# Mixture-of-experts stage: expert groups ordered from both ends of the load order, with odd pass counts and one shared turn

## The chip, the cores and the metric

The kernel runs on one core of one Trainium2 chip. The metric is the device time of one execution in microseconds (us), the median of several runs. All operands are 32-bit floats.

## The reference

A trunk of two layers (DEPTH = 2) works on 128 context tokens and 512 latent tokens, 640 in all, of width 1024. Each layer has a mixer (attention, a state-space scan, neighbourhood attention) and a channel sub-layer. The change lies in the channel sub-layer only, whose reference is:

```python
s = jax.nn.sigmoid((t @ p["w_router"]).astype(jnp.float32))
_, idx = lax.top_k(s + p["b_router"].astype(jnp.float32), TOP_K)          # 4 of 32 experts
sel = jnp.take_along_axis(s, idx, axis=-1)
w = sel / jnp.sum(sel, axis=-1, keepdims=True) * ROUTE_SCALE
gates = jnp.einsum("nk,nke->ne", w, jax.nn.one_hot(idx, N_EXPERTS))
hg = jnp.einsum("nd,edf->nef", t, p["w_e_gate"])                          # d = 1024, f = 128
hu = jnp.einsum("nd,edf->nef", t, p["w_e_up"])
routed = jnp.einsum("nef,efd->nd", jax.nn.silu(hg) * hu * gates[:, :, None], p["w_e_down"])
shared = (jax.nn.silu(t @ p["w_s_gate"]) * (t @ p["w_s_up"])) @ p["w_s_down"]
```

A layer has 640 x 4 = 2560 assignments of a token to an expert. How they fall follows from the drawn inputs. If the 32 experts of a layer are sorted by their number of tokens and taken four at a time, the most loaded expert of each four (its lead) has, from the reference's own routing:

| rank of the group | 0 | 1 | 2 | 3 | 4 | 5 | 6 | 7 |
|---|---|---|---|---|---|---|---|---|
| lead's tokens, layer 0 | 176 | 121 | 109 | 84 | 69 | 59 | 48 | 37 |
| lead's tokens, layer 1 | 274 | 123 | 104 | 77 | 67 | 58 | 49 | 27 |

## The kernel before, in words

Each layer runs its stages one after another; the channel sub-layer is `stage_tail` and then `stage_combine`. `stage_tail` first does the output projection, the second norm and the router. Then VectorE alone works out the routing (from line 2842 to line 2960): the mask of chosen experts, the loads `n_of`, each expert's `rank` by load, its `group` (rank // 4), its `lane` in the group (rank % 4), the number of turns `t_of` that it needs, and from these two tables of tokens by slot (`table`, `dest`), made by a matmul of 20 steps on TensorE (line 2611).

**A pass** handles 128 rows: 32 rows (GRAIN) for each of the four experts of a group (LANES), side by side on the array. **A turn** is two passes (UNROLL), so it handles up to 64 rows (PER_TURN) of each expert of its group. A group takes ceil(lead / 64) turns, and at least one. In a turn TensorE does, in this order: `up` of both passes (line 2640: 32 products of each pass, each with a weight load; an f32 product leaves two records), `turn_hidden` (a transpose, line 2647), `turn` of the first pass of the next turn (eight transposes of gathered rows, line 2627), `down` of pass 0 (line 2658), and again transpose, `turn` and `down` for pass 1. ScalarE and VectorE empty PSUM (lines 2749, 2755, 2760, 2766 and 2972, 2978, 2989).

**The rows.** GpSimd gathers the tokens of a pass from DRAM by an indirect DMA (line 2451) a turn ahead, and scatters the results by another (line 2463). Slots without a token move nothing.

**The weights.** An expert has three matrices of 1024 x 128, loaded by SyncE: gate and up (line 2414) and down (line 2419), 12 DMAs a group. There are two sets of SBUF slots, one for even and one for odd positions in the order. The loads for position s wait until the group at position s - 2 has done its last `up` (for gate and up), and then its last `down` (for down):

```python
if s >= 2:
    passed = turns(sp, s - 2)
    sp.wait_ge(sem("tile_up"), passed * UNROLL)
for c in range(LANES):
    load_up(s, c, which[c])
if s >= 2:
    sp.wait_ge(sem("tile_down"), passed * UNROLL)
```

TensorE waits for the gate and up weights of a group ahead of its first turn, and for the down weights ahead of each first `down`. The engines read the turn counts from a row of words (`m.words`), written when the routing is known; word P + s is the number of turns up to and with position s.

**The order of the groups** before the change: position of a group of rank g is 3g mod 8 (STRIDE = 3, lines 2903 to 2906). The ranks come in the order 0, 3, 6, 1, 4, 7, 2, 5, with 3, 2, 1, 2, 2, 1, 2, 1 turns in layer 0 (14) and 5, 2, 1, 2, 2, 1, 2, 1 in layer 1 (16).

`stage_combine` loads the scattered rows again, and begins when all are stored.

Of the kernel before, what the change touches and what calls it, by code (L numbers as in the profile page):

```python
# [16 lines left out]
ALU = mybir.AluOpType  # L17
# [38 lines left out]
LANES = 4  # L56
GRAIN = P // LANES
GROUPS = NE // LANES
STRIDE = 3
N_CHOICE = TOP_K * TILES  # L60
PER_TURN = UNROLL * GRAIN
MAX_TURNS = 2 * TOK // PER_TURN + GROUPS
TABLE = UNROLL * MAX_TURNS + 4
EVEN = 12582912.0
NO_ROW = 4096.0
# [2255 lines left out]
def stage_tail(nc, cx, L, m, x):  # L2321
# [5 lines left out]
    with ExitStack() as st:  # L2327
        def sb(name, shape, dt=F32):
            return st.enter_context(nc.sbuf_tensor(f"{name}_{L}", shape, dt))
# [18 lines left out]
        tiny = sb("route_tiny", [P, 12])  # L2348
        top = sb("route_top", [P, TILES, 8])
        small = sb("route_small", [P, 4, TILES])  # L2350
        cnt = sb("route_cnt", [P, 9, NE])
        ids = sb("route_ids", [P, 2])
        where = sb("route_where", [P, N_CHOICE, TABLE])
        silu = sb("ex_silu", [P, 2, P])
# [25 lines left out]

        def turns(eng, s):

            return eng.value_load(m.words[0:1, P + s:P + s + 1], min_val=s + 1, max_val=MAX_TURNS)

        def at(n, i):

# [111 lines left out]
        def _(pe):  # L2498
# [120 lines left out]
            def turn(n, i=0):  # L2619
                b = n % 2  # L2620
                pe.wait_ge(sem(f"xg_ready{b}"), i * (16 * UNROLL // 2) + 16 * (n // 2 + 1))
                if n:

                    pe.wait_ge(sem("xT_low"), at(n, i))
                    pe.wait_ge(sem("xT_high"), at(n, i))
                for k in range(KT):
                    ins = pe.transpose(ps[:, k // 4, (k % 4) * P:(k % 4 + 1) * P], xg[:, b, k * P:(k + 1) * P],
                                       cx.ident)
                ins.then_inc(sem("x_turned"), 1)

            def up(n, i, s):

                b = n % 2
                pe.wait_ge(sem("xT_low"), at(n + 1, i))
                pe.wait_ge(sem("xT_high"), at(n + 1, i))
                for k in range(KT):
                    for c in range(LANES):
                        rows = slice(c * GRAIN, (c + 1) * GRAIN)
                        ew = slots[LANES * (s % 2) + c][0].rearrange("p (g k f) -> p g k f", g=2, k=KT)
                        ins = pe.matmul(ps[rows, 2 + b, 0:2 * P].rearrange("p (g f) -> p g f", g=2), xT[:, b, k, rows],  # L2640
                                        ew[:, :, k, :], start=(k == 0), stop=(k == KT - 1))
                ins.then_inc(sem("tile_up"), 1)

            def turn_hidden(n, i):
                b = n % 2
                pe.wait_ge(sem("tile_hid"), at(n + 1, i))
                pe.transpose(ps[:, 2 + b, 2 * P:3 * P], hid[:, b, :], cx.ident).then_inc(sem("hid_turned"), 1)

            def down(n, i, s):

                b = n % 2
                pe.wait_ge(sem("hidT_out"), at(n + 1, i))
                pe.wait_ge(sem("y_low"), at(n + 1, i))
                pe.wait_ge(sem("y_high"), at(n + 1, i))
                for h in range(2):
                    for c in range(LANES):
                        rows = slice(c * GRAIN, (c + 1) * GRAIN)
                        ins = pe.matmul(ps[rows, 4 + 2 * b + h, :], hidT[:, b, rows],  # L2658
                                        slots[LANES * (s % 2) + c][1][:, h * SEC:(h + 1) * SEC], start=True, stop=True)
                ins.then_inc(sem("tile_down"), 1)  # L2660
# [3 lines left out]
            turn(1)  # L2664
            pe.wait_ge(sem("experts_known"), 1)
            pe.wait_ge(sem("shared_hid"), 2)
            first = 0
            for s in range(GROUPS):
                last = turns(pe, s)
                pe.wait_ge(sem(f"up_full{s % 2}"), 2 * LANES * 16 * (s // 2 + 1))  # L2670
                with pe.Fori(first, last) as i:
                    up(0, i, s)
                    up(1, i, s)
                    turn_hidden(0, i)
                    turn(2, i)
                    pe.wait_ge(sem(f"down_full{s % 2}"), LANES * 16 * (s // 2 + 1))
                    down(0, i, s)
                    turn_hidden(1, i)
                    turn(3, i)
                    down(1, i, s)  # L2680
                first = last

        @block.scalar
# [104 lines left out]
        def _(dve):  # L2788
# [96 lines left out]
            def whole(out, x, a, b):  # L2885

                step(dve, dve.tensor_scalar(out, x, a, b, ALU.mult, ALU.add))
                step(dve, dve.tensor_scalar(out, out, EVEN, None, ALU.add))
                step(dve, dve.tensor_scalar(out, out, -EVEN, None, ALU.add))

            n_of, key, rank, group, lane, t_of, lead, begin, tmp = (cnt[:, j, :] for j in range(9))
            wide = place.rearrange("p n s -> p (n s)")[:, 0:NE * NE].rearrange("p (a b) -> p a b", a=NE)

            step(dve, dve.scalar_tensor_tensor(out=key, in0=n_of, scalar=float(NE), in1=iota[:, 0:NE], op0=ALU.mult,
                                               op1=ALU.subtract))
            step(dve, dve.tensor_tensor(wide, spread(key, 1, NE), spread(key, 2, NE), ALU.is_gt))
            dve.tensor_reduce(rank, wide, AX.X, ALU.add)
            whole(t_of, n_of, 1.0 / PER_TURN, (PER_TURN - 1.0) / (2 * PER_TURN))
            step(dve, dve.tensor_scalar(t_of, t_of, 1.0, None, ALU.max))
            whole(group, rank, 1.0 / LANES, -(LANES - 1.0) / (2 * LANES))  # L2900
            step(dve, dve.scalar_tensor_tensor(out=lane, in0=group, scalar=-float(LANES), in1=rank, op0=ALU.mult,
                                               op1=ALU.add))
            whole(tmp, group, STRIDE / GROUPS, -(GROUPS - 1.0) / (2 * GROUPS))
            dve.tensor_scalar(group, group, float(STRIDE), None, ALU.mult)
            step(dve, dve.tensor_scalar(tmp, tmp, -float(GROUPS), None, ALU.mult))
            step(dve, dve.tensor_tensor(group, group, tmp, ALU.add))
            step(dve, dve.scalar_tensor_tensor(out=rank, in0=group, scalar=float(LANES), in1=lane, op0=ALU.mult,
                                               op1=ALU.add))
            step(dve, dve.scalar_tensor_tensor(out=lead, in0=lane, scalar=0.0, in1=t_of, op0=ALU.is_equal,
                                               op1=ALU.mult))  # L2910
            rows_high(TILES - 1)
# [5 lines left out]
            dve.tensor_reduce(ids[:, 1:2], pick[:, 0, 1, :], AX.X, ALU.add).then_inc(sem("ids_ready"), 1)  # L2917

            step(dve, dve.tensor_tensor(wide, spread(group, 1, NE), spread(group, 2, NE), ALU.is_lt))
            step(dve, dve.tensor_tensor(wide, wide, spread(lead, 1, NE), ALU.mult))  # L2920
            step(dve, dve.tensor_reduce(begin, wide, AX.X, ALU.add))
            step(dve, dve.tensor_scalar(tmp, lane, FAR, None, ALU.mult))
            step(dve, dve.scalar_tensor_tensor(out=begin, in0=begin, scalar=float(PER_TURN), in1=tmp, op0=ALU.mult,
                                               op1=ALU.add))
            dve.wait_ge(sem("ids_turned"), 1)
            dve.tensor_copy(m.words[:, :], ps[0:1, 7, 0:2 * P]).then_inc(sem("experts_known"), 1)
# [465 lines left out]
```

## Time and profile before

| | |
|---|---|
| median of 3 runs | 2555.4 us (2551.98 to 2559.52) |
| the profiled execution's own time | 2552.58 us |
| its span, first to last instruction | 2550.8 us |
| TensorE busy | 2374.8 us, 93% |
| VectorE busy | 938.5 us, 37% |
| ScalarE busy | 647.4 us, 25% |
| GpSimd busy | 412.6 us, 16% |
| mean granted TensorE clock | 0.972 |
| bytes moved by DMA | 368.37 MB, 144 GB/s over the span |

One profiled execution is read. Times are us from its start. PE is TensorE, DVE VectorE, ACT ScalarE, POOL GpSimd, SP SyncE; SPq is the queue in which SyncE issues its DMAs. "L2640" is line 2640 of the kernel. The products of the four lanes overlap, so the busy time of a group of them is less than count times mean.

### The profile page before, as it was taken

The page shows a single profiled execution, that of the slowest core. Times are in us where ns is not written, and L with a number is a line of the kernel's source. Part 1 is how long each engine was busy: PE and PEld are TensorE (multiplying, and loading weights), DVE is VectorE, ACT ScalarE, POOL GpSimd, SP SyncE. Part 2 cuts the span into 40 slices and gives each one's busy share as a digit, 9 for nine tenths or more (in the row PEclk, how much of TensorE's full clock was granted, in tenths as well). Part 3 has the DMA queues.
Part 4 walks back from the last instruction along what each step waited for, and adds up shares of the span by engine and source line. Part 5 has one row for each costly group of instructions (what it writes and reads, how often), then busy time and mean ns, then how long its engine had stood idle before and what let it go on. Part 6 is the DMA issues. An engine that isn't in the chain of part 4 may idle for free. (4 is left out here: it accounts for less than half of the span.)

```text
span 2550.8 us, 36359 instructions
## 1 busy us (share of the span) xinstructions
PE 2374.8 (93%) x13824; PEld 1413.1 (55%) x13824; DVE 938.5 (37%) x1813; ACT 647.4 (25%) x1574; POOL 412.6 (16%) x488
## 2 busy tenths in 40 slices
PE   7999999999998999899879999999999899989995
PEld 4446644566457655555455565556655765555552
DVE  2513412552007334422365153246300743452226
ACT  2224401450015013022132252037001501302221
POOL 0003100030003300133410030002100230013333
PEclk8999999999999999899989999999999999989997
DMA  9443145100644220689652220220042322065985
GB/s 348 173 164 102 58 169 214 42 1 33 213 137 110 72 70 34 262 328 401 250 216 88 87 104 33 85 74 1 33 131 76 107 86 70 34 234 207 374 333 221
DMA packets 170190, 368.37 MB, mean 144 GB/s; under 512 B 38836, under 2 KB 52156, under 8 KB 170052
## 3 DMA queue, kind: packets, MB, share of 16 engines
q1 hardware_dynamic: 121604, 261.23, 27.9%
q10 hardware_dynamic: 24768, 54.82, 6.1%
q0 software_dynamic: 23680, 50.43, 5.9%
q8 instruction: 91, 1.49, 0.2%
q14 instruction: 47, 0.39, 0.0%
HBM read 343.99 MB, written 47.56 MB: 154 GB/s over the span
## 5 line engine op out<-in xcount | busy, mean ns | idle before, releaser
L224 PE MATMUL ps<-hT,ring 128*128 128x512 f32 x496 | 222.9, 603 | 5.6 <-PEq L1242 2.7
L233 PE MATMUL ps<-ring,hT 128*128 128x512 f32 x480 | 213.5, 602 | 5.6 <-PEq L1286 4.4
L2640 PE MATMUL ps<-ring,mixT 128*32 128x256 f32 x2688 | 212.5, 379 | 0.6 <-DMA ring<-in_w_e_up 0.4
L2640 PEld LDWEIGHTS ps<-ring,mixT 128*32 128x32 f32 x2688 | 119.4, 110 | 92.9 <-issue 18.1
L224 PEld LDWEIGHTS ps<-hT,ring 128*128 128x128 f32 x496 | 92.8, 192 | 124.0 <-issue 123.9
L233 PEld LDWEIGHTS ps<-ring,hT 128*128 128x128 f32 x480 | 90.8, 192 | 117.8 <-issue 115.9
L1389 PE MATMUL ps<-late,ring 128*128 128x320 f32 x512 | 144.1, 440 | 3.7 <-PEq L1907 2.5
L2508 PE MATMUL ps<-ring,mixT 128*128 128x512 f32 x320 | 140.4, 598 | 4.4 <-PEq L1286 4.4
L1389 PEld LDWEIGHTS ps<-late,ring 128*128 128x128 f32 x512 | 98.1, 193 | 47.6 <-issue 8.2
L756 PE MATMUL ps<-hT,ring 128*128 128x512 f32 x256 | 114.5, 601 | 2.9 <-ACT ssm_dec L1011 2.9
L2658 PE MATMUL ps<-ring,ex_hidT 128*32 128x512 f32 x768 | 115.4, 598 | 0.8 <-DMA ring<-in_w_e_down 0.8
L2010 PE MATMUL ps<-hT,ring 128*128 128x512 f32 x256 | 113.3, 595 | 0.3 <-issue 0.3
L1352 PE MATMUL ps<-mix_T,mix_S 128*128 128x320 f32 x384 | 107.2, 434 | 1.8 <-POOL mix_S L1340 1.2
L2508 PEld LDWEIGHTS ps<-ring,mixT 128*128 128x128 f32 x320 | 60.8, 192 | 79.1 <-issue 79.1
L1949 POOL DMA_DIRECT2D na_raw<-rpb_scratch x64 | 38.1, 598 | 398.9 <-DVE na_bias L2250 291.0
L1352 PEld LDWEIGHTS ps<-mix_T,mix_S 128*128 128x128 f32 x384 | 72.5, 190 | 34.3 <-POOL mix_S L1340 2.2
L1580 POOL TENSOR_SCALAR da_co<-da_sm,da_rc,da_ls 128x1 f32<-128x1 f32 x32 | 11.0, 344 | 480.3 <-DVE da_rc L1864 480.3
L2978 DVE TENSOR_TENSOR ex_hid<-ps,ex_silu 128x128 f32<-128x128 f32 x60 | 17.5, 292 | 188.3 <-ACT ex_silu L2755 188.3
L2640 PE MATMUL ps<-hT,mixT 128*32 128x256 f32 x768 | 85.0, 379 | 0.0
L2640 PE MATMUL ps<-out_xn,mixT 128*32 128x256 f32 x384 | 84.8, 379 | 0.0
L756 PEld LDWEIGHTS ps<-hT,ring 128*128 128x128 f32 x256 | 48.2, 192 | 58.0 <-issue 57.9
L2010 PEld LDWEIGHTS ps<-hT,ring 128*128 128x128 f32 x256 | 47.4, 190 | 58.2 <-issue 58.2
(487 smaller groups left out, 4152.0 us busy)
## 6 DMA issues: line engine op xcount, KB each, us to landing
ring<-in_w_in SPq DMA_DIRECT2D x18, 2048.0 KB, 9.4
ring<-in_w_gate SPq DMA_DIRECT2D x12, 2048.0 KB, 8.7
ring<-in_w_e_down SPq DMA_DIRECT2D x48, 512.0 KB, 14.3
ring<-in_w_e_gate SPq DMA_DIRECT2D x40, 512.0 KB, 7.3
ring<-in_w_e_up SPq DMA_DIRECT2D x40, 512.0 KB, 8.4
mixT<-in_w_ada ACTq DMA_DIRECT2D x8, 2048.0 KB, 8.6
da_ada_w<-in_w_ada ACTq DMA_DIRECT2D x8, 2048.0 KB, 8.6
co_yg<-y_rows SPq DMA_DIRECT2D x28, 512.0 KB, 5.7
```

The costliest lines, as they stand in the source:

```text
L224: pe.matmul(lat, wide[:, k, c], hT[:, k, CTX:TOK], start=(k == 0), stop=(k == kt_n - 1))
L233: last = pe.matmul(out, cx.hT[:, k, tok(t)], wide[:, k, :], start=(k == 0), stop=(k == KT - 1))
L756: ins = pe.matmul(ps[:, 6, :], wide[:, k, (m % 4) * P:(m % 4 + 1) * P], cx.hT[:, k, CTX:TOK], start=(k == 0), stop=(k == KT - 1))
L1352: ins = pe.matmul(ps[:, bank(q, i), 0:HALF], left[:, k, :], right[:, k, :], start=(k == 0), stop=(k == KH - 1))
L1389: ins = pe.matmul(ps[:, BR + 2 * c + x, 0:HALF], wb[:, k, (2 * q + c) * P:(2 * q + c + 1) * P], cx.oT[:, k, half], start=(k == 0), stop=(k ...
L1580: pool.tensor_scalar(co[:, u % 2:u % 2 + 1], sm[:, u % 3, 0:1], rc[:, u % 3, 1:2], ls[:, 5:6], ALU.mult, ALU.mult).then_inc(sem("da_co"), 1)
L1949: eng.dma_start(raw[:, n % 4, :], src).then_inc(sem(f"na_raw{n % 4}"), 16)
L2010: ins = pe.matmul(ps[:, n % 2, :], wide[:, k, (n // 2) * P:(n // 2 + 1) * P], cx.hT[:, k, CTX:TOK], start=(k == 0), stop=(k == KT - 1))
L2508: ins = pe.matmul(ps[:, 2 * (t % 2) + n, :], cx.mixT[:, k, tok(t)], wide[n][:, k, :], start=(k == 0), stop=(k == KT - 1))
L2640: ins = pe.matmul(ps[rows, 2 + b, 0:2 * P].rearrange("p (g f) -> p g f", g=2), xT[:, b, k, rows], ew[:, :, k, :], start=(k == 0), stop=(k ...
L2658: ins = pe.matmul(ps[rows, 4 + 2 * b + h, :], hidT[:, b, rows], slots[LANES * (s % 2) + c][1][:, h * SEC:(h + 1) * SEC], start=True, stop= ...
L2978: dve.tensor_tensor(hid[:, b, :], ps[:, 2 + b, P:2 * P], silu[:, b, :], ALU.mult).then_inc(sem("tile_hid"), 1)
```

## The change

Four edits, all in `stage_tail` and its constants.

1. **Odd pass counts.** The groups of rank 3 and 4 get an odd number of passes: 2t + 1 with t = max(1, ceil((lead - 32) / 64)). The other groups keep 2t.
2. **Order.** A group of rank g goes to position min(2g, 15 - 2g): the ranks come in the order 0, 7, 1, 6, 2, 5, 3, 4.
3. **The shared turn.** Between the turns of position 6 and those of position 7 TensorE does one turn whose pass 0 is position 6's and whose pass 1 is position 7's. It stands in the code a second time, outside the loops, with waits for position 7's weights ahead of its second `up` and of its second `down`. All counts of turns for position 7 grow by one.
4. **Tables.** `begin` is counted in passes, not turns; MAX_TURNS grows by one (the tables of 60 columns, TABLE, become 62), and `cnt` has two more rows.

```diff
-STRIDE = 3
+ODD = (GROUPS // 2 - 1, GROUPS // 2)
+MIXED = GROUPS - 2
-MAX_TURNS = 2 * TOK // PER_TURN + GROUPS
+MAX_TURNS = 2 * TOK // PER_TURN + GROUPS + 1
...
-            return eng.value_load(m.words[0:1, P + s:P + s + 1], min_val=s + 1, max_val=MAX_TURNS)
+            n = eng.value_load(m.words[0:1, P + s:P + s + 1], min_val=s + 1, max_val=MAX_TURNS - 1)
+            return eng.snap(n + 1) if s > MIXED else n
...
+            def both(i, s, z):
+
+                up(0, i, s)
+                if z != s:
+                    pe.wait_ge(sem(f"up_full{z % 2}"), 2 * LANES * 16 * (z // 2 + 1))
+                up(1, i, z)
+                turn_hidden(0, i)
+                turn(2, i)
+                pe.wait_ge(sem(f"down_full{s % 2}"), LANES * 16 * (s // 2 + 1))
+                down(0, i, s)
+                turn_hidden(1, i)
+                turn(3, i)
+                if z != s:
+                    pe.wait_ge(sem(f"down_full{z % 2}"), LANES * 16 * (z // 2 + 1))
+                down(1, i, z)
...
                 with pe.Fori(first, last) as i:
-                    up(0, i, s)
-                    up(1, i, s)
...
-                    down(1, i, s)
+                    both(i, s, s)
+                if s == MIXED:
+                    both(last, s, s + 1)
+                    last = pe.snap(last + 1)
                 first = last
...
-            dve.tensor_reduce(rank, wide, AX.X, ALU.add)
-            whole(t_of, n_of, 1.0 / PER_TURN, (PER_TURN - 1.0) / (2 * PER_TURN))
+            step(dve, dve.tensor_reduce(rank, wide, AX.X, ALU.add))
+            step(dve, dve.tensor_scalar(odd, rank, LANES * ODD[0] - 0.5, None, ALU.is_gt))
+            step(dve, dve.scalar_tensor_tensor(out=odd, in0=rank, scalar=LANES * (ODD[1] + 1) - 0.5, in1=odd,
+                                               op0=ALU.is_lt, op1=ALU.mult))
+            step(dve, dve.scalar_tensor_tensor(out=t_of, in0=odd, scalar=-float(GRAIN), in1=n_of, op0=ALU.mult,
+                                               op1=ALU.add))
+            whole(t_of, t_of, 1.0 / PER_TURN, (PER_TURN - 1.0) / (2 * PER_TURN))
             step(dve, dve.tensor_scalar(t_of, t_of, 1.0, None, ALU.max))
+            dve.scalar_tensor_tensor(out=passes, in0=t_of, scalar=float(UNROLL), in1=odd, op0=ALU.mult, op1=ALU.add)
...
-            whole(tmp, group, STRIDE / GROUPS, -(GROUPS - 1.0) / (2 * GROUPS))
-            dve.tensor_scalar(group, group, float(STRIDE), None, ALU.mult)
-            step(dve, dve.tensor_scalar(tmp, tmp, -float(GROUPS), None, ALU.mult))
-            step(dve, dve.tensor_tensor(group, group, tmp, ALU.add))
+            step(dve, dve.tensor_scalar(tmp, group, -2.0, 2.0 * GROUPS - 1.0, ALU.mult, ALU.add))
+            step(dve, dve.scalar_tensor_tensor(out=group, in0=group, scalar=2.0, in1=tmp, op0=ALU.mult, op1=ALU.min))
...
+            dve.scalar_tensor_tensor(out=passes, in0=lane, scalar=0.0, in1=passes, op0=ALU.is_equal, op1=ALU.mult)
...
-            step(dve, dve.tensor_tensor(wide, wide, spread(lead, 1, NE), ALU.mult))
+            step(dve, dve.tensor_tensor(wide, wide, spread(passes, 1, NE), ALU.mult))
...
-            step(dve, dve.scalar_tensor_tensor(out=begin, in0=begin, scalar=float(PER_TURN), in1=tmp, op0=ALU.mult,
+            step(dve, dve.scalar_tensor_tensor(out=begin, in0=begin, scalar=float(GRAIN), in1=tmp, op0=ALU.mult,
```

## Rows read from the trace of the kernel before

**Rows 1.** The page: TensorE's share of the span; GB/s in 40 equal slices.

```profile
PE 2374.8 (93%) x13824; PEld 1413.1 (55%) x13824; DVE 938.5 (37%) x1813; ACT 647.4 (25%) x1574; POOL 412.6 (16%) x488
GB/s 348 173 164 102 58 169 214 42 1 33 213 137 110 72 70 34 262 328 401 250 216 88 87 104 33 85 74 1 33 131 76 107 86 70 34 234 207 374 333 221
```

**Rows 2.** Timeline of PE, second turn of layer 0: start us, us, instruction.

```profile
1079.75 7.09 PE L2640 MATMUL ps<-ring,mixT 128*32 128x256 f32 x128
...
1092.63 0.61 PE L2640 MATMUL ps<-ring,mixT 128*32 128x256 f32 x8
```

**Rows 3.** The page's costliest groups: one such DVE operation for each pass.

```profile
L2978 DVE TENSOR_TENSOR ex_hid<-ps,ex_silu 128x128 f32<-128x128 f32 x60 | 17.5, 292 | 188.3 <-ACT ex_silu L2755 188.3
```

**Rows 4.** What PE waited for in the expert turns, layer 0 and then layer 1.

```profile
PE ps L2627 <- DMA mixT<-h_rows,ex_index: 4.8, 4, 1.9
...
PE ps L2640 <- DMA ring<-in_w_e_up: 0.4, 1, 0.4
...
PE ps L2627 <- DMA mixT<-h_rows,ex_index: 4.3, 3, 2.3
```

**Rows 5.** Busy time by stretch of the expert turns; then PEclk, DMA share, GB/s.

```profile
1138.70:1188.20 49.50, 48.22 (x656) 25.73 (x658) 13.11 (x23) 13.00 (x32) 18.73 (x32) 1.00 1.03 411
1191.70:1235.20 43.50, 41.52 (x559) 22.71 (x557) 11.03 (x20) 11.06 (x27) 15.07 (x26) 1.00 1.00 391
1125.80:1241.10 115.30, 112.04 (x1526) 60.52 (x1528) 29.87 (x53) 29.71 (x71) 42.99 (x71) 1.00 0.96 379
1211.80:1238.40 26.60, 25.83 (x356) 14.71 (x360) 6.40 (x12) 6.39 (x16) 9.04 (x15) 1.00 0.90 358
...
2341.70:2357.50 15.80, 15.80 (x205) 8.24 (x204) 4.34 (x8) 4.34 (x11) 5.83 (x10) 1.00 0.89 343
2380.40:2429.90 49.50, 48.37 (x660) 25.80 (x662) 13.12 (x23) 13.21 (x32) 19.00 (x32) 1.00 1.02 408
2433.20:2473.90 40.70, 40.70 (x555) 21.91 (x557) 11.04 (x20) 11.00 (x27) 14.89 (x25) 1.00 1.01 398
```

**Rows 6.** DMA queues in a window around each layer's expert turns: GpSimd's queue.

```profile
q0 software_dynamic: 8640, 20.99, 19.1%
...
q0 software_dynamic: 9792, 20.99, 23.5%
```

**Rows 7.** Timeline of SP: first gate issue of position 2, by layer; position 5's first and last.

```profile
1099.92 0.33 SPq L2414 DMA_DIRECT2D ring<-in_w_e_gate  x1
...
2341.74 0.33 SPq L2414 DMA_DIRECT2D ring<-in_w_e_gate  x1
...
1165.93 0.34 SPq L2414 DMA_DIRECT2D ring<-in_w_e_gate  x1
...
1169.41 1.02 SPq L2414 DMA_DIRECT2D hT<-in_w_e_up  x1
```

**Rows 8.** DMA issues: KB each, us to landing; the issue of 1169.41, that of 2345.75.

```profile
hT<-in_w_e_up SPq DMA_DIRECT2D x1, 512.0 KB, 18.8
...
ring<-in_w_e_up SPq DMA_DIRECT2D x1, 512.0 KB, 11.7
```

**Rows 9.** Timeline of PE: first product after the expert turns, by layer, idle before.

```profile
1261.29 2.04 PE L3039 MATMUL ps<-shared_down,shared_hidden 128*128 128x512 f32 x2 [9.80 <-PEq L2327]
...
2500.96 2.04 PE L3039 MATMUL ps<-shared_down,shared_hidden 128*128 128x512 f32 x2 [10.46 <-PEq L2327]
```

**Rows 10.** Stretches by window: PE idle for 4.5 us before 352.9, and what follows.

```profile
348.40:352.20 3.80, 0.00 (x0) 0.00 (x0) 0.00 (x0) 0.60 (x1) 0.00 (x0) 1.00 1.07 393
352.20:355.60 3.40, 2.71 (x16) 0.59 (x16) 0.17 (x1) 0.00 (x0) 0.00 (x0) 0.50 0.65 224
```

**Rows 11.** Timelines of DVE and PE in layer 0's routing.

```profile
1024.23 0.18 DVE L2887 TENSOR_SCALAR route_cnt<-route_cnt 128x32 f32<-128x32 f32 x1
...
1025.41 0.19 DVE L2907 SCALAR_TENSOR_TENSOR route_cnt<-route_cnt 128x32 f32<-128x32 f32 x1
...
1041.86 1.51 PE L2611 MATMUL ps<-route_where,late 128*128 128x60 f32 x6 [4.03 <-DVE late L2943]
```

More of the change, by code:

```diff
@@ L2350, in stage_tail @@
         small = sb("route_small", [P, 4, TILES])
-        cnt = sb("route_cnt", [P, 9, NE])
+        cnt = sb("route_cnt", [P, 11, NE])
         ids = sb("route_ids", [P, 2])
@@ L2671, in _ @@
                 with pe.Fori(first, last) as i:
-                    up(0, i, s)
-                    up(1, i, s)
[L2674 to L2679, printed above, removed]
-                    down(1, i, s)
+                    both(i, s, s)
+                if s == MIXED:
+                    both(last, s, s + 1)
+                    last = pe.snap(last + 1)
                 first = last
@@ L2889, in whole @@
                 step(dve, dve.tensor_scalar(out, out, -EVEN, None, ALU.add))
-            n_of, key, rank, group, lane, t_of, lead, begin, tmp = (cnt[:, j, :] for j in range(9))
+            n_of, key, rank, group, lane, t_of, lead, begin, tmp, odd, passes = (cnt[:, j, :] for j in range(11))
             wide = place.rearrange("p n s -> p (n s)")[:, 0:NE * NE].rearrange("p (a b) -> p a b", a=NE)
```

## The prediction

> **What bounds the kernel now.** I read the page first: TensorE is busy for 93% of the span, and the DMA rate is low in most slices but near 400 GB/s in a few [rows 1]. An average like this says "TensorE-bound", so a pass less looks like time gained; but the change touches one stage, run once a layer, and its limits must be read there. So next I read one turn in TensorE's timeline [rows 2]. From the first `up` at 1079.75 to the next at 1092.63 a turn takes 12.88 us, with no idle time: 7.1 us for both `up`s, and two blocks of transposes and `down`. One VectorE operation at line 2978 stands for each pass, 60 in all [rows 3]: 30 turns of two passes, as the leads give (14 and 16). In layer 0 TensorE waited once for gate and up weights, for 0.4 us, and in layer 1 for no weights at all; for gathered rows it waited 4.8 and 4.3 us [rows 4]. So before the change TensorE bounds the expert turns, narrowly.
>
> How narrowly is in the rows by stretch [rows 5]. In four long stretches in which loads of weights were always pending, the DMA engines ran at a busy share of 1.0 and moved 411, 391, 408 and 398 GB/s, 402 on average. The stage has two limits that nearly touch, and the change moves only one of them: it removes TensorE work and not a byte of traffic. Weights are 12 x 0.524 = 6.29 MB for a group (512 KB each) [rows 8], whatever its turns; and GpSimd's queue moved 20.99 MB in either layer [rows 6], which is 2560 rows of 4 KB, in and out, and follows the assignments, not the passes.
>
> **Part 1, the passes.** By the leads, rank 3 and 4 (84 and 69 tokens; 77 and 67) needed two turns each, 4 passes, and now need 3. The turns by position become 3, 1, 2, 1, 2, 1, 1, shared, 1 in layer 0 (13) and 5, 1, 2, 1, 2, 1, 1, shared, 1 in layer 1 (15). TensorE's work falls by one turn a layer: 2 x 12.88 = 25.8 us if nothing else ended last. No lead is near 96 or 64 (84, 69, 77, 67), so no group gets more passes.
>
> **Part 2, the order, and what the loads do.** A group's loads of gate and up start when the group two positions ahead has done its last `up`, that is 12.88 - 7.1 = 5.8 us before the next group starts. If the group between has one turn, the load has 5.8 + 12.9 = 18.7 us. Position 5's load in layer 0, made while the previous one was still landing, shows what it needs: issued from 1165.93, last issue 1169.41, landed 18.8 us after that, at 1188.2: 22.3 us [rows 7, 8]. Before, it had two turns to hide in. After, positions 2, 4 and 6 have the short window (behind one-turn groups), and position 7 is wanted in the second pass of the shared turn. Position 2 finds the queue empty, which takes under 16 us (below), and so fits; the others don't. Each group with a single turn asks for 6.29 MB and 1.6 MB of rows in 12.88 us, 612 GB/s, which is beyond 411. So from position 2 on I price the stage by bytes.
>
> Position 2's load starts where it does now, at 1099.92 and 2341.74 [rows 7], since the first group is unchanged; position 1's was issued long before, and its window only shrinks at its far end. From there until TensorE can do the shared turn's second `up`, the queues must move six loads of gate and up (6 x 4.19) and five of down (5 x 2.10), 35.6 MB, and the rows of some nine turns: 9 x 20.99/13 = 14.5 MB in layer 0, 9 x 20.99/15 = 12.6 MB in layer 1. Loads never run dry: when TensorE has got position 4's weights, its next request comes 20 us later, and by then 6.29 + 2.10 MB are still to be moved. At 402 GB/s that is 50.2/0.402 = 124.9 us, and 48.2/0.402 = 120.0 us. For start and landing I add 2.5 us: a load by itself, from 2341.74 to 2345.75 + 11.7 = 2357.45 [rows 8], ran for 15.7 us at 343 GB/s, 13.3 us' worth at 408. The second `up` of the shared turn then starts at 1227.3 and 2464.2. Behind it stand 12.88 - 3.55 of its own turn and one turn, 22.2 us, so the turns end at 1249.5 and 2486.4. Before, they ended at 1261.29 - 9.80 = 1251.5 and 2500.96 - 10.46 = 2490.5 [rows 9]. **Gain: 2.0 + 4.1 = 6.1 us**, of 25.8. TensorE's removed work turns into waits for weights, ahead of positions 4 and 6 and in the shared turn: some 15 us in layer 0 and 11 in layer 1.
>
> Bounds: at 411 in both layers, 122.1 and 117.4 us, the gain is 4.8 + 6.7 = 11.5 us. At 379, which is the mean over a long stretch with pauses (1125.8 to 1241.1), 132.5 and 127.2 us, it is a loss of 5.6 + 3.1 = 8.7 us. I take 402, the mean of the four stretches without pauses, because the after has none.
>
> Queued behind the new waits: on TensorE nothing can pass them. On SyncE the down loads of s wait for `tile_down` of s - 2 as before. GpSimd's gathers are issued one turn ahead and gain slack when TensorE waits, so the waits for rows (4.8 and 4.3 us) don't grow.
>
> **Part 3, the clock.** The new waits are longer than any now in the stage (all stretches of rows 5 show clock 1.00). What an idle TensorE costs is seen elsewhere: in 348.4 to 352.2 it did nothing, and in the 3.4 us after that the granted clock was 0.50, 1.2 GHz instead of 2.4 [rows 10]. Work in 3.4 us at half clock comes 1.7 us late. Ahead of positions 4 and 6 this is absorbed by the pending loads; in the shared turn it lands on the path. **Loss: 2 x 1.7 = 3.4 us**; bounds 0 (no drop) and 6.8.
>
> **Part 4, the routing on VectorE.** TensorE waited 4.03 us for this chain ahead of the table [rows 11], so all of it is on the path. The six operations from 1024.23 to 1025.41 (1.18 us) go; seven of the same kind come, five at 0.21 us from start to start and two without a wait of about 0.15, 1.35 us; the reduction of `rank` now is waited for (0.1), and the flags of 62 instead of 60 columns add 3% of 1.4 us. **Loss: about 0.3 to 0.4 us a layer, 0.8 in all.** The later issue of the first weights by 0.4 us is hidden (they land over 10 us before their use). The matmul table's two columns and the code of the extra turn, which is read in a straight line, I take at nothing; the cover of the latter is TensorE's wait for weights, and without it the price is some tenths.
>
> **Sum:** -6.1 + 3.4 + 0.8 = -1.9 us against the profiled execution's 2552.6 (span 2550.8 and 1.8 around it). That execution is 2.8 us under the median of 2555.4, so the median comes to 2553.5, say 2554. Less than 0.3% (7.7 us) either way is what a measurement of this kernel can't tell from no change.
>
> **Rivals.** (a) *The loads are hidden and the removed turns count in full:* -25.8 + 0.8, 2530 us. For it: today a one-turn group at position 2 or 5 costs nearly nothing [rows 4]. Against it: those stand alone between longer groups, and 612 GB/s is beyond all rows. Chance 0.10. (b) *Bytes decide, but the queues run at their best rate and the clock stays:* -11.5 + 0.8, 2545 us. For it: 411 and 408 in two stretches of 50 us. Chance 0.17. (c) *Slower: without pauses the queues deliver less.* The place is the shared turn's wait, and the chain is the same sum. It decides below 387 GB/s: there the loads' term is +3.5 us, and with the other two terms the sum passes 7.7. At 379, with the clock's upper bound: +8.7 + 6.8 + 0.8 = +16, 2572 us. For it: 391 and 398 in the stretches where two one-turn loads followed, with the last pieces of a load coming in late. Its extreme is the 358 GB/s of 1211.8 to 1238.4: 140.2 and 134.6 us, +24 for the loads, 2583 us; against that, the stretch holds the end of the loads. Chance 0.16 together. (d) *The change doesn't shorten anything because counts differ from the leads:* then about 2556; 60 passes in the trace agree with the leads. Chance 0.02.
>
> The Trainium skill speaks for (c): its page "DMA: Bandwidth & Descriptors", "Where 436 GB/s comes from", says that HBM-to-SBUF transfers are bound by a per-core HBM share of about 358 GB/s, while loads by a core alone measure up to 425. By the first figure the sum would be that of the extreme of (c), 2583. The trace agrees with the second: 411 GB/s over 49.5 us [rows 5], on a chip where this core works alone.
>
> **How the numbers follow.** The forecast has a chance of 0.55. Faster: (a) + (b) = 0.27. Slower: (c) = 0.16. Same: 0.55 + 0.02 = 0.57. The range leaves out (a) and the tail of (c): from 2540, below (b) and its lower clock and rate ends, to 2568, near (c). The forecast's own range is 2548 to 2562.
>
> **What would show it.** In the profile after: 56 operations at line 2978 (26 and 30 passes); waits of TensorE at line 2640 for the DMA of gate or up weights, three a layer, of 3 to 7 us each, some 25 us in total; the DMA share near 1.0 from position 2's load to the shared turn, at 395 to 411 GB/s; clock 0.50 somewhere behind a wait. It would be wrong if the turns took 12.88 us throughout and no wait for weights showed (a), or if the stretch without pauses ran under 387 GB/s (c).

## The result, and the profile after

| | before | after |
|---|---|---|
| median | 2553.4 us (5 runs, 2545.8 to 2559.5) | 2566.1 us (5 runs, 2563.4 to 2569.7) |
| ratio | 1 | 1.0044, 95% interval 1.0023 to 1.0065 |
| profiled execution, its span | 2552.6 us, 2550.8 us | 2566.8 us, 2565.0 us |
| TensorE busy in the span | 2374.8 us | 2366.2 us |
| mean granted clock | 0.972 | 0.964 |

The changed kernel is slower: by 0.44%, some 11 us, by the ratio, and by 12.7 us between the two medians. A second set gave 2564.7 us and a ratio of 1.0034 (after_again, below). TensorE's products at line 2640 (now 2642) fell as they should, from 3840 records to 3584, and its idle time and half clock grew by more.

The page after: the groups of the `up` products that read the first slots, of the gathered rows' transposes, and VectorE's one operation a pass.

```profile
L2642 PE MATMUL ps<-ring,mixT 128*32 128x256 f32 x2720 | 209.3, 390 | 23.3 <-DMA ring<-in_w_e_up 13.1
L2996 DVE TENSOR_TENSOR ex_hid<-ps,ex_silu 128x128 f32<-128x128 f32 x56 | 16.3, 292 | 210.0 <-ACT ex_silu L2768 210.0
L2629 PE MATMUL ps<-base,mixT 128*128 128x128 f32 x480 | 62.9, 274 | 13.4 <-DMA mixT<-h_rows,ex_index 10.6
```

The second row answers to [rows 3]: 56 passes, not 60. The first shows what came in their place: 23.3 us idle ahead of `up`, ended by DMAs of gate and up weights (13.1 for this slot set alone), and a mean of 390 ns where a product takes 379 at full clock.

What TensorE waited for in the expert turns, first layer 0, then layer 1 (total, times, longest); this answers to [rows 4]:

```profile
PE ps L2642 <- DMA ring<-in_w_e_up: 7.1, 1, 7.1
PE ps L2642 <- DMA hT<-in_w_e_up: 6.5, 1, 6.5
PE ps L2629 <- DMA mixT<-h_rows,ex_index: 5.1, 4, 2.6
PE ps L2660 <- DMA ring<-in_w_e_down: 1.0, 1, 1.0
...
PE ps L2642 <- DMA ring<-in_w_e_up: 6.0, 2, 3.7
PE ps L2629 <- DMA mixT<-h_rows,ex_index: 5.5, 5, 2.6
PE ps L2642 <- DMA hT<-in_w_e_up: 3.1, 1, 3.1
```

That is 14.6 us of waits for weights in layer 0 and 9.1 in layer 1. Before, it was 1.2 and none: the 0.4 us of [rows 4] and, in the kernel before,

```profile
PE ps L2658 <- DMA ring<-in_w_e_down: 0.8, 1, 0.8
```

Gathered rows cost 0.3 and 1.2 us more than before.

Stretches by window: the columns are those of [rows 5], ending in granted clock, DMA share and GB/s. The first is from about the start of position 2's loads in layer 0 to the shared turn's second `up`; then three parts of it; then three stretches at half clock; then the same whole in layer 1 and the last of that layer's three half-clock stretches.

```profile
1100.20:1233.60 133.40, 116.25 (x1562) 62.33 (x1554) 30.16 (x54) 30.10 (x72) 44.14 (x72) 0.96 0.99 390
1150.00:1186.00 36.00, 28.68 (x380) 15.31 (x376) 6.70 (x12) 6.69 (x16) 9.92 (x18) 0.91 1.01 401
1186.00:1196.00 10.00, 10.00 (x134) 5.17 (x126) 3.12 (x6) 3.20 (x8) 3.62 (x6) 1.00 0.86 335
1196.00:1233.60 37.60, 29.15 (x412) 16.13 (x404) 7.23 (x14) 7.11 (x18) 12.08 (x19) 0.94 1.02 402
...
1164.30:1171.10 6.80, 3.13 (x32) 1.78 (x36) 0.00 (x0) 0.00 (x0) 0.55 (x1) 0.50 1.03 415
1229.20:1239.40 10.20, 5.76 (x56) 3.14 (x60) 0.00 (x0) 0.00 (x0) 0.00 (x0) 0.50 0.57 230
...
1075.60:1079.00 3.40, 3.40 (x20) 1.09 (x13) 0.85 (x2) 0.77 (x3) 1.02 (x1) 0.50 1.03 419
...
2351.20:2479.40 128.20, 117.00 (x1547) 62.77 (x1539) 30.14 (x54) 30.11 (x72) 43.97 (x72) 0.97 1.01 398
2478.40:2485.30 6.90, 5.90 (x56) 3.16 (x60) 0.00 (x0) 0.00 (x0) 0.00 (x0) 0.51 0.41 165
```

The DMA share is 0.99 and 1.01 over the two whole stretches, with one drop to 0.86 in layer 0: the queues, not TensorE, set the pace. And the clock is 0.50 behind each of the three longest waits in layer 0, in stretches in which TensorE was busy for 3.13, 5.76 and 3.40 us: half of that, 6.1 us, is lost in layer 0. Two of the stretches begin while TensorE still waits, so their lengths are longer than the work in them.

The shared turn in TensorE's timeline, start and length in us; and the first product of the combining stage of either layer, which answers to [rows 9]:

```profile
1233.64 0.61 PE L2642 MATMUL ps<-ring,mixT 128*32 128x256 f32 x1 [6.54 <-DMA hT<-in_w_e_up]
1240.22 1.04 PE L2629 MATMUL ps<-base,mixT 128*128 128x128 f32 x8
...
1268.46 2.04 PE L3057 MATMUL ps<-shared_down,shared_hidden 128*128 128x512 f32 x2 [9.49 <-PEq L2328]
...
2514.90 2.04 PE L3057 MATMUL ps<-shared_down,shared_hidden 128*128 128x512 f32 x2 [10.11 <-PEq L2328]
```

The expert turns of layer 0 ran from 1064.03 to 1268.46 - 9.49 = 1258.97: 194.9 us, where they took 187.8 (1063.74 to 1251.5). In layer 1 it is 215.7 against 211.2 us. The account of layer 0: a turn less -12.9, waits for weights +13.4, for rows +0.3, half clock +6.1, together +6.9 of the measured +7.1. Layer 1: -12.9 + 9.1 + 1.2 and three half-clock stretches with 12.5 us of work in them, +6.2, make +3.6 of +4.5. The rest of the span's 14.2 us is 0.3 ahead of layer 0's turns and 2.3 between the two stages, of which the routing is 0.4; for the other 1.9 I have no cause, and that part differs by several us between the other runs as well.

### The profile page after: what moved, and what is told of

Its sections match the earlier page's. It is cut to its first block and busy times, and to the rows that moved or that the text cites. A ratio compares the mean times of both kernels' runs of the same rounds, so it can differ in the third digit from the quotient of the medians.

```text
span 2565.0 us, 35495 instructions
## 1 busy us (share of the span) xinstructions
PE 2366.2 (92%) x13468; PEld 1408.1 (55%) x13468; DVE 932.0 (36%) x1803; ACT 640.7 (25%) x1558; POOL 402.8 (16%) x472
## 5 line engine op out<-in xcount | busy, mean ns | idle before, releaser
L2642 PE MATMUL ps<-ring,mixT 128*32 128x256 f32 x2720 | 209.3, 390 | 23.3 <-DMA ring<-in_w_e_up 13.1
L1390 PEld LDWEIGHTS ps<-late,ring 128*128 128x128 f32 x512 | 99.0, 194 | 48.2 <-issue 9.4
L2660 PE MATMUL ps<-ring,ex_hidT 128*32 128x512 f32 x752 | 109.0, 606 | 1.0 <-DMA ring<-in_w_e_down 1.0
L2629 PE MATMUL ps<-base,mixT 128*128 128x128 f32 x480 | 62.9, 274 | 13.4 <-DMA mixT<-h_rows,ex_index 10.6
L1353 PE MATMUL ps<-hT,ring 128*128 128x320 f32 x256 | 73.3, 440 | 1.4 <-PEq L1517 1.4
```

The costliest lines, as they stand in the source:

```text
L1353: ins = pe.matmul(ps[:, bank(q, i), 0:HALF], left[:, k, :], right[:, k, :], start=(k == 0), stop=(k == KH - 1))
L1390: ins = pe.matmul(ps[:, BR + 2 * c + x, 0:HALF], wb[:, k, (2 * q + c) * P:(2 * q + c + 1) * P], cx.oT[:, k, half], start=(k == 0), stop=(k ...
```

## The experiments

Two theories stand against each other. Theory "bytes": single-turn groups ask for more than the queues move, and what is lost is waits for weights plus the clock behind them. The rival "shared turn" puts the loss on the extra turn and its surroundings. Each ratio is to runs of before on the same chip.

**order_only_b.** The kernel before with the new order alone.

```diff
-            whole(tmp, group, STRIDE / GROUPS, -(GROUPS - 1.0) / (2 * GROUPS))
-            dve.tensor_scalar(group, group, float(STRIDE), None, ALU.mult)
-            step(dve, dve.tensor_scalar(tmp, tmp, -float(GROUPS), None, ALU.mult))
-            step(dve, dve.tensor_tensor(group, group, tmp, ALU.add))
+            step(dve, dve.tensor_scalar(tmp, group, -2.0, 2.0 * GROUPS - 1.0, ALU.mult, ALU.add))
+            step(dve, dve.scalar_tensor_tensor(out=group, in0=group, scalar=2.0, in1=tmp, op0=ALU.mult, op1=ALU.min))
```

> The kernel before with the new order alone: every group keeps its even number of passes (14 and 16 turns), no shared turn. Theory 'bytes' (single-turn groups at positions 1, 3, 5 give the loads behind them only 18.7 us where they need some 22): TensorE waits for the weights of positions 4 and 6, and the kernel is slower than before, by 6 to 12 us (2560 to 2566). Rival 'shared turn' (the loss comes from the extra turn itself: its code outside the loop, its longer routing, its half clock): no shared turn, so the time of before, 2553 within 3.

Measured: 2577.4 us, ratio 1.0107 (1.0081 to 1.0132), 27 us slower. "Bytes" has the sign, "shared turn" falls; but the size is more than double the top of what I had expected. So the new order is what costs, and the passes removed with it gave some 16 to 19 us of their 25.8 back (ratios 1.0107 against 1.0044 and 1.0034, from different sets). TensorE's waits in layer 0, the product behind the long one in the timeline, and the window at half clock:

```profile
PE ps L2640 <- DMA ring<-in_w_e_up: 6.4, 1, 6.4
PE ps L2627 <- DMA mixT<-h_rows,ex_index: 5.0, 5, 2.1
...
1166.78 8.44 PE L2640 MATMUL ps<-ring,mixT 128*32 128x256 f32 x100 [6.37 <-DMA ring<-in_w_e_up]
...
1165.80:1172.60 6.80, 5.82 (x56) 3.14 (x60) 0.00 (x0) 0.00 (x0) 0.00 (x0) 0.50 1.03 412
```

One wait a layer (6.4 and 5.0 us, at position 4), and 5.8 us of `up` at half clock right behind it, which costs another 2.9. The expert turns of the two layers grew by some 19 us together, the span of this execution by 24; for the other 5 us, outside the turns, I have no cause.

**half_before_b and half_after_b.** In both, the loads for positions 2 to 7 bring only the first half of each weight matrix's columns; the other half of a slot keeps an earlier group's weights, so half of those weights doesn't enter the computation.

```diff
+                    n = D if s < 2 else D // 2
-                    sp.dma_start(up_to[:, i2 * D:(i2 + 1) * D],
+                    sp.dma_start(up_to[:, i2 * D:i2 * D + n],
...
+                n = D if s < 2 else D // 2
-                sp.dma_start(slots[LANES * (s % 2) + c][1], w["w_e_down"].rearrange("l e f d -> (l e) f d")[
+                sp.dma_start(slots[LANES * (s % 2) + c][1][:, 0:n], w["w_e_down"].rearrange("l e f d -> (l e) f d")[
```

> The kernel before, in which the loads of positions 2 to 7 bring only half of each weight matrix (the other half of a slot keeps older weights), so half of the expert weights is not loaded. Theory 'bytes': the few waits in the expert turns go (3 to 4 us), 2548 to 2551. Rival 'shared turn': the same. It is the partner for half_after_b.

> The changed kernel with the same halved loads of positions 2 to 7. Theory 'bytes': with the loads hidden, one turn a layer less comes out in full: 25.8 us minus 0.8 us of routing under half_before_b, so 2523 to 2527, no wait of TensorE for gate or up weights and clock 1.00 in the expert turns. Rival 'shared turn': the loss stays when the loads are short, so 2550 or more.

Measured: 2549.4 us for the first (ratio 0.9989, 0.9975 to 1.0004), 2519.7 for the second (0.9874, 0.9849 to 0.9900). The difference is 29.7 us, and by the ends of the two intervals it can be anything from some 19 to 40; 25.0 were expected. In the two traces the expert turns shrank by 12.4 and 9.2 us, 21.6 of 25.8. So with the loads out of the way, the change gives most or all of what it removes. Passes are 60 and 56 here too. The group of the `up` products, first of half_before_b, then of half_after_b:

```profile
L2642 PE MATMUL ps<-ring,mixT 128*32 128x256 f32 x2688 | 212.5, 379 | 0.3 <-issue 0.3
```

```profile
L2644 PE MATMUL ps<-ring,mixT 128*32 128x256 f32 x2720 | 198.4, 379 | 0.3 <-issue 0.3
```

There is no wait for weights, and 379 ns, in both. The clock was to stay at 1.00: in half_after_b it fell once, to 0.50 for 3.4 us at 2279.1 in layer 1, behind a wait for rows of 2.4 us. The extra turn's code, its place outside the loop and the longer routing are in half_after_b as they are in the changed kernel, so they aren't the cause of the loss.

**odd_early_b, plain_early and odd_spread.** Other orders, which keep all bytes. The position of a rank is read from a small constant table: PLACES = (5, 2, 3, 0, 1, 4, 6, 7) for the first two (ranks 3, 4, 1, 2, 5, 0, 6, 7), (1, 3, 4, 5, 6, 0, 2, 7) for the third (ranks 5, 0, 6, 1, 2, 3, 4, 7). MIXED is the position whose last pass is in the shared turn, 0 in odd_early_b and 5 in odd_spread; the loads two positions behind it now also wait for that pass. plain_early is the kernel before with the order alone.

```diff
-MIXED = GROUPS - 2
+MIXED = 0
+PLACES = (5, 2, 3, 0, 1, 4, 6, 7)
...
                     passed = turns(sp, s - 2)
-                    sp.wait_ge(sem("tile_up"), passed * UNROLL)
+                    free = sp.snap(passed * UNROLL + 1) if s - 2 == MIXED else passed * UNROLL
+                    sp.wait_ge(sem("tile_up"), free)
...
-            step(dve, dve.tensor_scalar(tmp, group, -2.0, 2.0 * GROUPS - 1.0, ALU.mult, ALU.add))
-            step(dve, dve.scalar_tensor_tensor(out=group, in0=group, scalar=2.0, in1=tmp, op0=ALU.mult, op1=ALU.min))
+            step(dve, dve.tensor_tensor(wide8, spread(group, 2, GROUPS), spread(iota[:, 0:GROUPS], 1, NE), ALU.is_equal))
+            step(dve, dve.tensor_tensor(wide8, wide8, spread(iota[:, P + N_CHOICE + 1:P + N_CHOICE + 1 + GROUPS], 1, NE),
+                                        ALU.mult))
+            step(dve, dve.tensor_reduce(group, wide8, AX.X, ALU.add))
```

> The changed kernel with the same odd passes and the same one shared turn, but the two middle ranks first: ranks in the order 3, 4, 1, 2, 5, 0, 6, 7, so turns 1, shared, 1, 2, 2, 1, then the longest group, 1, 1. All bytes and all TensorE work as in the changed kernel; the routing has one VectorE operation more of 0.3 us. Theory 'bytes': the loads run ahead behind the two-turn groups, most of the 25.8 us comes out: 2530 to 2542. Rival 'shared turn': as the changed kernel, 2566 within 4.

> The kernel before (even passes, no shared turn) with the ranks in the order of odd_early_b: 3, 4, 1, 2, 5, 0, 6, 7, so 2, 2, 2, 2, 1, 3 or 5, 1, 1 turns. Theory 'bytes': TensorE bounds nearly all of it, one wait ahead of the longest group and little else: the time of before within 4, 2549 to 2556, and odd_early_b gains on it only a part of 25.8 us because its own loads take over. Rival 'the place of the groups decides nothing by itself': the same as order_only_b, 2577.

> The changed kernel's odd passes and one shared turn with the ranks in the order 5, 0, 6, 1, 2, 3, 4, 7, so turns 1, the longest group, 1, 2, 2, 1, shared, 1, 1. A load behind a single-turn group follows a longer group, in which the queues ran empty. Theory 'bytes': one wait in the first turns (position 1's weights land at about 1083, are wanted at 1080) and one at the shared turn; 2536 to 2546, like odd_early_b or some us better. Rival 'only an order with the middle ranks at the start or the end works': 2550 or more.

Measured: odd_early_b 2543.9 us (0.9971, 0.9953 to 0.9989); plain_early 2554.8 us (0.9998, 0.9981 to 1.0015); odd_spread **2537.3 us** (0.9925, 0.9901 to 0.9948). The first is 2 us over its expected stretch, the others inside theirs. With the same products, the same bytes and the same one shared turn, the order alone moves the time from 2566 to 2537 (ratios 1.0044 and 0.9925). Plain_early, with TensorE's full work, is the time of before, where the same even passes in the order from both ends (order_only_b) took 2577. What TensorE waited for, in odd_early_b's layer 0, in its layer 1, and in odd_spread's layer 0 and layer 1:

```profile
PE ps L2645 <- DMA hT<-in_w_e_up: 3.7, 1, 3.7
PE ps L2645 <- DMA ring<-in_w_e_up: 0.7, 1, 0.7
...
PE ps L2645 <- DMA hT<-in_w_e_up: 4.6, 1, 4.6
```

```profile
PE ps L2645 <- DMA hT<-in_w_e_up: 3.0, 1, 3.0
PE ps L2645 <- DMA ring<-in_w_e_up: 1.9, 1, 1.9
...
PE ps L2645 <- DMA hT<-in_w_e_up: 1.8, 1, 1.8
...
PE ps L2645 <- DMA ring<-in_w_e_up: 0.2, 1, 0.2
```

4.9 us of such waits in layer 0 and 2.0 in layer 1, where the changed kernel had 13.6 and 9.1.

**busy.** The changed kernel, with transposes of no use in its long waits.

```diff
+            def spare(n):
+                for _ in range(n):
+                    pe.transpose(ps[:, 3, 3 * P:4 * P], cx.ident, cx.ident)
...
                 up(0, i, s)
                 if z != s:
+                    spare((34, 14)[L])
                     pe.wait_ge(sem(f"up_full{z % 2}"), 2 * LANES * 16 * (z // 2 + 1))
...
                 last = turns(pe, s)
+                spare({4: (36, 10), 6: (0, 16)}.get(s, (0, 0))[L])
```

> The changed kernel, in which TensorE fills most of its long waits for weights with transposes of the identity matrix into an unused stretch of PSUM: 34 (layer 0) and 14 (layer 1) of 0.13 us ahead of the wait in the shared turn, 36 and 10 ahead of position 4, 16 ahead of position 6 in layer 1. Nothing else changes; the waits end when they did. Theory 'the clock falls behind the waits and costs about 3 us a layer in the shared turn': the granted clock stays at 1.00 there, the second up takes 3.5 instead of 6.5 us, 4 to 8 us faster than the changed kernel: 2558 to 2562. Rival 'the clock lost there is given back, since the DMA queues bound the stage': as the changed kernel, 2566 within 2.

Measured: 2560.6 us, ratio 1.0033 (1.0018 to 1.0048). That is 4.1 and 5.5 us under the changed kernel's two medians, but its interval overlaps both of theirs (after_again: 1.0018 to 1.0050), so as a time it is inconclusive. The profile is clearer. Windows over the shared turns, and VectorE's operation of both passes in layer 0's:

```profile
1228.00:1243.00 15.00, 15.00 (x196) 9.74 (x188) 2.66 (x6) 2.75 (x8) 3.67 (x6) 1.00 0.55 221
2481.00:2493.00 12.00, 12.00 (x173) 6.59 (x175) 3.25 (x6) 3.23 (x8) 3.99 (x9) 1.00 0.16 57
...
1231.43 0.29 DVE L3002 TENSOR_TENSOR ex_hid<-ps,ex_silu 128x128 f32<-128x128 f32 x1 [3.07 <-ACT ex_silu L2774]
1238.89 0.29 DVE L3002 TENSOR_TENSOR ex_hid<-ps,ex_silu 128x128 f32<-128x128 f32 x1 [7.17 <-ACT ex_silu L2774]
```

The clock stays at 1.00, and the two are 7.46 us apart. The same two operations of the changed kernel:

```profile
1227.48 0.29 DVE L2996 TENSOR_TENSOR ex_hid<-ps,ex_silu 128x128 f32<-128x128 f32 x1 [3.07 <-ACT ex_silu L2768]
1240.50 0.29 DVE L2996 TENSOR_TENSOR ex_hid<-ps,ex_silu 128x128 f32<-128x128 f32 x1 [12.72 <-ACT ex_silu L2768]
```

13.02 us apart, for a wait of 6.5 and a second `up` at half clock. Not all of the 5.6 us between the two is the clock. These are the spare transposes of the two shared turns:

```profile
1230.98 3.93 PE L2671 MATMUL ps<-base 128*128 128x128 f32 x34
...
2472.41 1.75 PE L2671 MATMUL ps<-base 128*128 128x128 f32 x14
```

In layer 0 they and the wait together took 3.8 us, not 6.5: 2.7 us of the 5.6 are a shorter wait, with 3.3 us of wait now ahead of position 6, where there was none; the other 2.9 us are the clock. In layer 1 position 7's last piece had landed at 2470.3 (issued at 2454.6, 15.7 us), ahead of the transposes, which there only cost 1.7 us. So the expectation that the waits would end when they did was wrong. What the run does show is the link of idle time and clock: ahead of position 4 in layer 0, 4.15 us of transposes and 2.7 us of wait left the clock at 1.00, where the unfilled wait of 7.1 us had brought 0.50; and the wait ahead of position 6, which nothing filled, brought 0.50 for 3.4 us. An idle TensorE is what lowers the clock there, and keeping it busy keeps it up; what that is worth in the median isn't settled.

**fill.** The changed kernel, with the shared turn's first `down` ahead of its wait.

```diff
                 up(0, i, s)
-                if z != s:
-                    pe.wait_ge(sem(f"up_full{z % 2}"), 2 * LANES * 16 * (z // 2 + 1))
-                up(1, i, z)
+                if z == s:
+                    up(1, i, z)
                 turn_hidden(0, i)
                 turn(2, i)
                 pe.wait_ge(sem(f"down_full{s % 2}"), LANES * 16 * (s // 2 + 1))
                 down(0, i, s)
+                if z != s:
+                    pe.wait_ge(sem(f"up_full{z % 2}"), 2 * LANES * 16 * (z // 2 + 1))
+                    up(1, i, z)
...
                 silu_up(0, i)
-                silu_up(1, i)
                 hidden_out(0, i)
+                silu_up(1, i)
```

> The changed kernel, in which the shared turn does the transpose of the first pass's hidden rows, the turn of the next rows and the first down ahead of the wait for position 7's weights, not behind its second up (ScalarE takes the hidden rows of pass 0 ahead of the silu of pass 1). 3.2 us of TensorE work move into a wait of 6.5 us in layer 0 and of 3.1 us in layer 1. Theory 'bytes': what stood behind the landing shrinks by 3.2 us a layer, and the shorter idle time may spare some of the half clock: 5 to 10 us faster than the changed kernel, 2556 to 2561. Rival 'the landing itself moves' (the earlier rows traffic takes the queues from the weights): 2564 or more.

Measured: 2559.3 us, ratio 1.0018 (1.0006 to 1.0030): 5 to 7 us under the changed kernel's two medians, inside what "bytes" gave; but its interval overlaps both of theirs (1.0018 to 1.0050 and 1.0023 to 1.0065), so as a time it is inconclusive too. The shared turn of layer 0 in TensorE's timeline, its first `up`, its first `down` and the first product of its second `up`:

```profile
1223.50 3.64 PE L2642 MATMUL ps<-ring,mixT 128*32 128x256 f32 x64
...
1229.15 1.92 PE L2660 MATMUL ps<-ring,ex_hidT 128*32 128x512 f32 x16
...
1233.14 0.40 PE L2642 MATMUL ps<-ring,mixT 128*32 128x256 f32 x1 [2.08 <-DMA hT<-in_w_e_up]
```

The wait is 2.08 us instead of 6.54, the second `up` starts 133.1 us behind position 2's first issue, where it was 132.1, so the landing has hardly moved; its first product takes 0.40 us, not 0.61, so the clock is full, and less stands behind it. The turns of layer 0 took 190.6 us instead of 194.9. In layer 1 they took 215.5 instead of 215.7: the wait in the shared turn is gone there, but the clock fell behind a wait for rows of 3.7 us.

**after_again and odd_spread_fill.** The changed kernel unedited, and the edits of odd_spread and fill together, on one chip.

> The changed kernel once more, unedited, on the same chip and beside the same runs of before as odd_spread_fill, so that the two can be compared directly and the size of the loss is known from a second set: 2563 to 2569, 8 to 15 us over before. A theory that puts the loss down to the spread between chips or sets expects it within 4 us of before.

> odd_spread (ranks 5, 0, 6, 1, 2, 3, 4, 7, odd passes, one shared turn) with the shared turn of fill (first down ahead of the wait for the second group's weights). In odd_spread the shared turn waited 1.9 us in layer 0 and not in layer 1. Theory 'bytes': 2 us better in layer 0, and up to 1 us lost in layer 1, where the second pass's up now stands directly ahead of the transpose that needs it: 2534 to 2539, the time of odd_spread. Rival 'every wait counts at its length plus the clock': 2532 or less.

Measured: after_again 2564.7 us, before 2554.7, ratio 1.0034 (1.0018 to 1.0050): the loss stands, at its lower edge some 5 us. Its trace repeats the change's: 13.6 and 11.2 us of waits for gate and up weights, though in layer 1 they fall ahead of position 4 (6.2 us) and in the shared turn (5.0), and none ahead of position 6. odd_spread_fill 2539.1 us, ratio 0.9948 (0.9928 to 0.9969): no better than odd_spread, and at the upper edge of what "bytes" gave; where the waits are short there is little to fill.

## Why the prediction was wrong

The forecast was "no change" (2554, with 2540 to 2568), at 0.57; it came out slower, which had 0.16, though inside the stated range. The mechanism was the forecast's own: the removed work turned into waits for weights. Two terms were too small: the bytes that the queues must move ahead of the shared turn's second `up`, and the half clock.

- **The passes.** Right: 56 of them, and 12.88 us for a turn without a wait. half_after_b shows most or all of the gain once the loads are short, and no price for the extra turn's code; the "some tenths" that the prediction names for it is shown by no run.
- **Waits ahead of positions 4 and 6 and in the shared turn.** Right in kind. Layer 0: 7.1 at position 4 and 6.5 in the shared turn, and no such wait at position 6; with 1.0 us for down weights together 14.6 of "some 15". Layer 1: 9.1 of 11. That layer 0's sum fits is partly luck: the landing came 4.7 us later than priced, and waits for rows and half clock ahead of it, 1.6 us each, took up a part of that. The waits for rows, priced at no growth, grew by 0.3 and 1.2 us.
- **Rate of the queues, 402 GB/s.** Nearly right: 398 over all of layer 1, and 401 and 402 in two windows of layer 0, but 390 over all of it. The whole stretches of both layers are above the 387 below which (c) decides.
- **When position 7's weights land.** This step failed. I priced 127.4 us from position 2's first issue to the second `up` of the shared turn, and 122.5 in layer 1. Measured: from 1101.59 to 1233.64, 132.1 us, and from 2351.72 to 2479.40, 127.7 us: 5 us too little in either layer, and in after_again's trace it is 132.3 and 129.7. The rate was nearly right, the bytes were not. I had 50.2 and 48.2 MB: 35.6 of weights and 14.5 and 12.6 of rows. Here are the queue of the weights (q1) and that of the rows (q0) in exactly these two windows (packets, MB, share), each with the weights' queue behind it, until that was empty (up to 1245 and 2500):

```profile
q1 hardware_dynamic: 10181, 37.10, 70.8%
q0 software_dynamic: 5169, 14.48, 28.2%
q1 hardware_dynamic: 187, 0.66, 14.2%
...
q1 hardware_dynamic: 10241, 37.31, 73.6%
q0 software_dynamic: 5053, 13.54, 27.0%
q1 hardware_dynamic: 127, 0.45, 5.3%
```

The weights are 1.5 and 1.7 MB above the 35.6, and with the 0.66 and 0.45 that came after, these are the 2.10 MB of one group's down loads. So most of position 7's down loads moved ahead of the landing that TensorE waited for, and I had counted them behind it. The rows were as priced in layer 0 and 0.9 MB more in layer 1. With 0.2 MB of instructions the windows hold 51.8 and 51.0 MB, 1.6 and 2.8 more than priced, which at 402 GB/s is 3.9 and 7.0 us; layer 0's lower rate adds 3.3 and layer 1's 0.8, and the 2.5 us that I had added for start and landing comes off. The down loads are issued right behind the last piece of gate and up, which lands among them. Here is that last piece's issue in layer 0, the next one's, and how long the first took to land:

```profile
1212.53 2.10 SPq L2416 DMA_DIRECT2D hT<-in_w_e_up  x1
1214.72 1.95 SPq L2421 DMA_DIRECT2D ring<-in_w_e_down  x1
...
hT<-in_w_e_up SPq DMA_DIRECT2D x1, 512.0 KB, 20.9
```

- **"Loads never run dry."** False in one place of layer 0: 335 GB/s from 1186 to 1196. Position 6's first load was issued at 1189.70, 21.7 us behind the start of position 4's turns (1167.97) and not 20, since the half clock had stretched them. So the clock lost ahead of position 6 was not all absorbed by the pending loads. A sum in which the queues are always full leaves out that a slow TensorE also issues late.
- **The clock.** The mechanism was right, the term too small: 1.7 us a layer. Behind the last landing stood 25.3 us (1233.64 to 1258.97) and 25.4, not 22.2: 3.1 and 3.2 us a layer. I had taken 3.4 us of work at half clock; here it was 5.8 and 5.9 us of `up`, in stretches of 10.2 and 6.9 us that began during the wait. A further dip that I had not forecast fell in layer 0's first turn, behind a wait for rows of 2.6 us (1.9 before), and made that turn 1.4 us longer together with it. The Trainium skill, "TensorE: Matmul & The Clock Gate", in its section "HAM oscillation — how this bites in real kernels", tells of such a case: a DMA wait ahead of each tile makes the next one start cold. The trace agrees: 0.50 behind the waits for weights of 7.1, 6.5, 3.7, 3.1 and 2.3 us. The length of the wait alone doesn't decide it: behind one for rows of 2.57 us in layer 1 (2299.0) the clock stayed at 1.00.
- **The sum.** It was to be -1.9 us, and the span grew by 14.2. Of the 16.1 between, the late landings are 4.7 and 5.2, the half clock behind them gave 2.9 beyond the 3.4 priced, and 1.7 are the later first issue of position 2 in layer 0 (1101.59, it was 1099.92). The rest is the part between the stages.
- **The routing.** Right: the chain grew by 0.4 us, and TensorE's wait ahead of the table is 4.40 us instead of 4.03 [rows 11].
- **The rivals.** (c), slower, was the outcome in sign, but its reason, a lower rate, was not. By the account the waits alone are a draw in layer 0 (-12.9 + 13.4) and the half clock makes the loss. No run shows that kernel: in busy, where part of the half clock was gone (8.8 us of work at it in the expert turns instead of 24.8), it was still 0.33% slower than before. (a), the full gain, is refuted for this order, and half_after_b shows under which condition it would hold. The figure of about 358 GB/s, which the Trainium skill's page "DMA: Bandwidth & Descriptors", "Where 436 GB/s comes from", gives as the bound of a core's loads, didn't hold for this core alone: 398 GB/s over 128.2 us in layer 1.

## What to carry to other kernels

Ahead of removing work from the busiest engine of a stage, price the bytes of that stage against their rate. Price also what is issued behind the last load that is waited for: here about three quarters of it moved ahead of that load's landing. Where both limits nearly touch, mind the order: a short piece of work leaves little time to hide the load issued with it, so put a long piece ahead of it, in which the queues run empty. And a wait made by such a cut costs TensorE more than its length: behind the waits for weights here it did 3 to 6 us of work at half clock, which cost another 1.6 to 3 us each.

## What the runs showed of the hardware that I had not expected

A wait of 3.1 us in the middle of dense work (2476.3 to 2479.4) had more half clock behind it than one of 7.1 us: the stretches at 0.50 were 6.9 and 6.8 us long, but the first began 1.0 us before its wait ended and the second 3.7 us before, which leaves 5.9 and 3.1 us of work at half clock. The work lost did not follow the length of the wait. The order of the eight groups, with the same products and bytes, was worth 29 us of 2566, 1.1% (27 us against after_again).
